# Two decoder layers written out instead of looped, with the expert sum, the next norm and the final scaling done tile by tile

## What is computed

```python
for l in range(DEPTH):                                   # DEPTH = 2
    xp, ... = decoder_layer(xp, 0, ...)                  # 512 prompt rows
    xs, ... = decoder_layer(xs, PAST_LEN, ...)           # 32 sample rows
y_prompt, y_sample = rmsnorm(xp, final_g), rmsnorm(xs, final_g)

def decoder_layer(x, ...):
    h = rmsnorm(x, norm1_g)
    ... = split_cols(h @ w_in)                           # three token mixers:
    #  A gated MLP over chunks, B dilated window attention, C gated delta rule
    #  behind a short convolution over time (state_conv, c_conv_w)
    x = x + concat(out_a, out_b, out_c) @ w_out
    x = x + hier_moe(rmsnorm(x, norm2_g), ...)           # top 2 of 32 experts per token
    return x, ...

def rmsnorm(x, g):
    return x * rsqrt(mean(x * x, -1) + EPS) * g          # in float32
```

## Time and profile before

| | us |
|---|---|
| median of three runs | 1950.37 |
| the profiled execution | 1945.06 |
| its span, first to last instruction | 1943.1 |
| PE busy in it | 1553.9 (80%) |
| DVE, ACT, POOL busy | 621.2, 400.6, 169.7 |
| convR of layer 1 starts | 27.09 |
| first expert sum of layer 1, of layer 2 | 949.57, 1906.63 |
| convR of layer 2 starts | 982.47 |

### The profile page before, as it was taken

How to read it: one execution, slowest core, us unless ns; L and a number is a source line. 1 busy time by engine, 2 the same in 40 slices (tenths; PEclk the granted TensorE clock), 3 DMA queues, 4 the chain that set the end, 5 groups by cost and what they waited for, 6 DMA issues and landing times. The chain is left out here.

```text
span 1943.1 us, 31857 instructions
## 1 busy us (share of the span) xinstructions
PE 1553.9 (80%) x12956; PEld 1020.3 (53%) x12956; DVE 621.2 (32%) x1587; ACT 400.6 (21%) x955; POOL 169.7 (9%) x211
## 2 busy tenths in 40 slices
PE   6999978887679597878399998888785896978880
PEld 3476566765445354544155765667653454544450
DVE  2433155665113211111245322566541132111113
ACT  3221122322311111111131212223232110111111
POOL 0000000000000322222000000000000012222210
PEclk9999998895789699999799989889867897999995
DMA  7152010002862599999440511000047535999984
GB/s 274 45 177 80 1 36 2 2 18 58 226 236 79 170 390 394 397 395 401 151 143 10 189 58 35 2 2 2 20 121 223 197 124 216 387 398 394 397 336 155
DMA packets 97141, 337.13 MB, mean 174 GB/s; under 512 B 33325, under 2 KB 44941, under 8 KB 72317
## 3 DMA queue, kind: packets, MB, share of 16 engines
q1 hardware_dynamic: 77484, 307.86, 44.0%
q0 software_dynamic: 13296, 25.98, 3.9%
q10 hardware_dynamic: 6240, 1.57, 0.4%
HBM read 313.25 MB, written 37.83 MB: 181 GB/s over the span
## 5 line engine op out<-in xcount | busy, mean ns | idle before, releaser
L1587 PE MATMUL bank<-ring,proj_raw 128*64 128x256 f32 x2048 | 264.2, 411 | 79.9 <-DMA ring<-in_w 77.0
L1587 PEld LDWEIGHTS bank<-ring,proj_raw 128*64 128x64 f32 x2048 | 168.8, 143 | 156.2 <-issue 94.9
L1362 PE MATMUL bank<-ring,hT_raw 128*128 128x384 f32 (+2 forms) x768 | 229.2, 462 | 0.0
L1362 PEld LDWEIGHTS bank<-ring,hT_raw 128*128 128x128 f32 x768 | 149.0, 195 | 78.0 <-issue 4.8
L2175 DVE TENSOR_TENSOR qkv_raw<-qkv_raw,bank 128x128 f32<-128x128 f32 x64 | 18.4, 287 | 446.9 <-ACT qkv_raw L1022 446.9
L1299 PE MATMUL bank<-hT_raw,ring 128*128 128x512 f32 x288 | 127.6, 596 | 0.0
L1608 PE MATMUL bank<-ring,proj_raw 128*64 128x512 f32 x512 | 123.9, 604 | 1.5 <-issue 1.5
L1507 PE MATMUL bank<-ring,hT_raw 128*128 128x512 f32 x256 | 113.6, 597 | 0.0
L1080 PE MATMUL bank<-work 64*64 64x64 f32 (+1 forms) x1608 | 73.1, 256 | 37.6 <-DVE work L1730 26.2
L1574 PE MATMUL bank<-consts,proj_raw 64*128 64x64 f32 x512 | 70.1, 278 | 29.0 <-DMA proj_raw<-h_rows,idx 29.0
L1080 PEld LDWEIGHTS bank<-work 64*64 64x64 f32 (+1 forms) x1608 | 66.7, 168 | 47.0 <-DVE work L1730 29.5
(11 more groups left out here) (312 smaller groups left out, 1988.8 us busy)
## 6 DMA issues: line engine op xcount, KB each, us to landing
ring<-in_w SPq DMA_DIRECT2D x192, 1024.0 KB, 18.5
ring<-in_w_in SPq DMA_DIRECT2D x10, 1536.0 KB, 15.1
ring<-in_cache_win_k SPq DMA_DIRECT2D x16, 768.0 KB, 8.7
ring<-in_cache_win_v SPq DMA_DIRECT2D x16, 768.0 KB, 13.7
ring<-in_cache_win_k SPq DMA_DIRECT2D x16, 576.0 KB, 6.9
ring<-in_cache_win_v SPq DMA_DIRECT2D x16, 576.0 KB, 11.1
ring<-in_w_out SPq DMA_DIRECT2D x4, 2048.0 KB, 11.7
h_rows<-proj_raw SPq DMA_DIRECT2D x16, 512.0 KB, 3.6
```

Of the source, the lines that this page charges most:

```text
L1362: mm = pe.matmul(bank[0:ROWS[t], 0:w.shape[2]], hT[:, k, 128 * t:128 * t + ROWS[t]], w[:, k, :], start=k == 0, stop=k == KT - 1)
L1587: mm = pe.matmul(bank[CAP * j:CAP * j + CAP, 0:256].rearrange("p (w f) -> p w f", w=2), rowsT[k % 2][:, CAP * c:CAP * c + CAP], w13[:, :, ...
```

## The change

Each engine's program is written out for both layers, with a set of semaphores for each layer; `leave_layer` is gone. The entry into a norm is one routine on ACT and one on DVE that run tile by tile; it serves both layers and the final norm. On SP the first two `w_in` parts of layer 2 are loaded when experts 29 and 30 have left their slots, the third behind the ten gathers, and the taps and convolution state behind that, once tile 0's sum has read `got[0]` and `got[1]`. `final_g` is loaded ahead of the last gathers into another buffer, and each scaled tile has its own store. `hst` moves in `qkv_raw`. The expert loops, the projections and the mixers keep their code.

```diff
-        hst = [qkv_raw[:, D * i:D * i + D] for i in range(2)]
+        hst = [qkv_raw[:, D * (3 + i):D * (3 + i) + D] for i in range(2)]
-        g_final = proj_raw[:, 0:D]
+        g_final = work[:, 0:D]
-        def leave_layer(eng, L, clears=False):
-            eng.drain().then_inc(layer_left, 1)
-            eng.wait_ge(layer_left, (L + 1) * 5)
...
# SP
-            with sp.Fori(0, DEPTH) as L:
-                sp.dma_start(g1, lay["norm1_g"]...).then_inc(gain_loaded, 16)
-                sp.dma_start(state_rows[0:24, :], ...).then_inc(taps_loaded, 16)
-                sp.dma_start(state_rows[24:28, :], ...).then_inc(taps_loaded, 16)
-                for n in range(3):
-                    stream(L, n, loads[n](L, n % 3))
+            gain_load(0)
+            conv_loads(0)
+            for n in range(3):
+                stream(0, n, loads[n](0, n))
+            for L in range(DEPTH):
...
+                if L + 1 < DEPTH:
+                    gain_load(L + 1)
+                    for n in range(2):
+                        sp.wait_ge(s.act_filled, A0 + 2 * (NE - 3 + n) + 2)
+                        stream(L + 1, n, loads[n](L + 1, n))
+                else:
+                    sp.dma_start(g_final, ...).then_inc(fin_gain, 16)
+                dense_loads(sp, s, L)
                 for k in range(3):
+                    sp.wait_ge(rows_stored[k], 16 * (L + 1) * per_buffer[k] + 16)
                 for t in range(NT):
                     for k in range(2):
                         sp.dma_start(got[2 * t + k]..., y_rows...)
-                dense_loads(sp, L)
-                leave_layer(sp, L)
+                if L + 1 < DEPTH:
+                    stream(L + 1, 2, loads[2](L + 1, 2))
+                    sp.wait_ge(got_used, L * NT + 1)
+                    conv_loads(L + 1)
-            sp.wait_ge(fin_row, NT)
-            sp.dma_start(outs["y_prompt"]..., x[:, 0:NP, :])
+            for t in range(NT):
+                sp.wait_ge(fin_row, t + 1)
+                    sp.dma_start(outs["y_prompt"]...[t], x[:, t, :])
# ACT
+            def enter(L):
+                for t in range(NT + 1):
+                    if t < NT:
+                        if L:
+                            act.wait_ge(got_used, (L - 1) * NT + t + 1)
+                        act.activation(junk1..., x[0:ROWS[t], t, :], ACT.Square, accum_out=ssq...).then_inc(row_squared, 1)
+                    if t >= 1:
+                        u = t - 1
+                        act.wait_ge(row_asked, L * NT + u + 1)
+                        act.activation(rstd[:, u:u + 1], rstd[:, u:u + 1], ACT.Sqrt).then_inc(row_root, 1)
+                        if L < DEPTH:
+                            if u >= 2:
+                                act.wait_ge(of_layer[L].vec_filled, V_AT[("norm1", u - 2, 1)] + 1)
+                            act.activation(hst[u % 2]..., x[...], ACT.Copy, scale=rstd...).then_inc(of_layer[L].rows_ready, 1)
# PE
+                if L:
+                    pe.wait_ge(of_layer[L - 1].act_drained, A0 + 2 * NE)
+                    pe.wait_ge(of_layer[L - 1].vec_drained, V0 + 2 * NE)
# DVE
+            def joined(L, t):           # the two expert sums of tile t, each behind its gather
+            def asked_root(L, t):       # ssq of tile t to mean + EPS, reciprocal, row_asked
+            def enter(L, normed):
+                for t in range(NT + 2):
+                    if L and t < NT:
+                        joined(L - 1, t)
+                    if 1 <= t <= NT:
+                        asked_root(L, t - 1)
+                    if t >= 2:
+                        normed(t - 2)
...
+            enter(DEPTH, finished)      # finished(t): x times the root times final_g
```

More of the change, by code:

```diff
@@ L495, in build @@
+        of_layer = [Signals(L) for L in range(DEPTH)]
         a_jobs, v_jobs = schedule()
@@ L840, in _ @@
+            for L in range(DEPTH):
+                s = of_layer[L]
+                steps, roots, asked = [0], [0], [0]
+                enter(L)
                 bank = get(("tapsT",))
-                act.activation(taps, bank[:, 0:NCT * 28].rearrange("p (c n) -> p c n", c=NCT), ACT.Copy).then_inc(act_drained, 1)
+                act.activation(taps, bank[:, 0:NCT * 28].rearrange("p (c n) -> p c n", c=NCT), ACT.Copy).then_inc(s.act_drained, 1)
                 for i in range(NCT + 1):
```

744 lines of the change are left out of this document (363 added, 381 removed).

## The result

The changed kernel takes 1934.01 us (median of 5 runs, 1927.87 to 1938.93), the kernel before in the same series 1950.37 (5 runs, 1946.23 to 1954.27): a ratio of 0.9916, interval 0.9889 to 0.9942. It is faster by 16.4 us, where 11.8 was forecast, and 1934.01 lies in the range (1930.5 to 1944.0). A second series of both kernels gives a ratio of 0.9945, which is 10.7 us. The changed kernel's profiled execution took 1934.01 us too, with a span of 1932.2; 1933.3 was forecast for it.

A forecast was written before the change was run, and what follows sets the result against it. The prediction took the experts' up projection, waiting for expert weights, as costliest and unchanged. End 12.3, passage 0.6 and start -1.1 sum to 11.8 us: 1950.37 to 1938.6, range 1930.5 to 1944.

The forecast's parts named there:

- The end: First expert sum of layer 2 to the last row: running by tile gains 12.3 us, bounds 9 and 14.
- the 8.8: At the end, from sums' end to first scaling: 8.8 us of the gain, holding the meeting and final_g's load.
- the loop's jump: Between the layers: the jump's instruction fetch costs 3.9 us, won by written-out code but hidden behind the taps.
- The passage: First expert sum of layer 1 to convR of layer 2: gains 0.6 us, bounds -4 and +8.
- the landing of the taps: In the passage: taps, behind gathers and w_in, reach PE at 964.4 instead of 972.00.
- The bound of 4.6: Layer 1's last expert row store, slowed by w_in beside it: bounds 0 and 4.6 us, 0.8 taken.
- The clock: At convR of layer 2: a low clock would cost 1.4 us; half, 0.8, was counted.
- The start: Up to convR of layer 1: tile-wise order loses 1.1 us, bounds 0.5 and 2.
- The middles: Each layer's convR to its first expert sum, 922.5 and 924.2 us: zero change, 1.5 us either side.
- The passage flows: Rival, in the passage: taps early enough, DVE alone sets it, 24.5 us; total 1931; chance 0.18.
- Hand-overs cost: Rival: ACT and DVE requests per tile, 15 tiles, lose 4.5 us; 1945; chance 0.17 with no overlap at the end.
- A starved engine: Rival: written-out code's fetches late under expert loads, 4.6 us each time; four times give 1945 to 1957; chance 0.05.

The follow-up runs named there:

- Old_end: Changed kernel with only the end put back as before, but without the meeting; 1941.11 us, ratio 0.9976 to the kernel before.
- loads_behind: Changed kernel with taps and state right behind the ten gathers and all three w_in parts behind them; 1926.07 us, ratio 0.9899 to the kernel before.
- all_four: all_three plus the edit of sums_first, all ten DVE sums ahead of tile 0's gain; 1914.86 us, ratio 0.9837 to the kernel before.
- rep_after: The changed kernel run once more without any edit; 1932.75 us, ratio 0.9945 to the kernel before.
- sums_first: Changed kernel with all ten DVE sums and the means of tiles 0 to 3 ahead of tile 0's gain in the passage; 1927.84 us, ratio 0.9892.
- all_three: Changed kernel with early taps, all w_in parts behind the gathers, and all squares and root requests first at the start; 1920.34 us, ratio 0.9861.
- before_again: The kernel before, unchanged, profiled once more to see how its stages vary; 1943.32 us in one run.
- early_taps: Changed kernel with taps and convolution state loaded before the experts into a free buffer; 1921.11 us, ratio 0.9874 to the kernel before.
- all_three_again: all_three run once more without further edit; 1919.72 us, ratio 0.9876 to the kernel before.

## Why the prediction was right, and where it was not

**The end: right, and under-sized.** 12.3 forecast; 14.0 from the first sum (36.5 to 22.5), 14.5 from the last store. DVE's row of work was 20.1 us instead of 21.2, and the last store's end came 2.4 behind it instead of 3. The hops between dependent operations were free, which was my bound of 14. Old_end shows that both the meeting and the tiles count. But the meeting is worth 3 to 4.5 us, not the larger part of the 8.8 that I had put down to it and the load of `final_g`. No run separates the loop's jump, for which the prediction named 3.9 us, from the meeting.

**The passage: wrong in one step, the landing of the taps.** It was to gain 0.6 us and lost 5.1 from the last row store to convR. The step that failed is the time at which the taps reach PE. Predicted 964.4 - 943.24 = 21.2 us behind the last row store; measured 28.2. What follows the taps was right: 16.7 forecast, 16.2 measured (985.16 - 969.01), DVE's standstill before tile 3's sums included. The 7.0 us divide so:

- The gathers start 5.12 us behind the store's issue, I had 3.4: 1.8. The bound of 4.6 held; loads_behind shows 2.95 where no `w_in` flows.
- The gathers flow at 258 and 322 GB/s, where as far behind their start it was 338 and 412 before. Over eight us these are 0.68 MB less, at 412 GB/s 1.7 us.
- Then, from 959 to 965, `w_in` and what is left of the gathers move 221 and 287 GB/s at a DMA share above 1, where I had reckoned with the 365 of the earlier trace rows: 1.52 MB in 6 us instead of in 4.2, 1.8.
- The tail, state and taps behind `w_in` in small packets, share 0.77 and 214 GB/s in the last window: 1.7, which is not measured but what is left.

The rates are measured, their cause is not: no run changes the size of the packets alone. The low rate of the third stretch also shows in all_four (257 GB/s in 963:967, with no state or taps behind), so it isn't they who make it. The Trainium skill's rule that descriptors start in order within a queue ("DMA: Bandwidth & Descriptors", "Two DMAs through the same engine are not ordered") agrees with the traces: in the changed kernel, in rep_after and in sums_first the small taps land behind all of `w_in`. The order was right and the rates too high.

**The clock: half counted, twice the price.** I took 0.8, half of 1.4, for a low clock at convR. It was low in all nine executions whose passage ran tile by tile, and took 10.1 to 11.5 us from convR to the second long projection; it was full in all four where the transposes of at least three tiles ran in one piece (both of before, sums_first, all_four), which took 8.7. That is 1.4 to 2.8 us, mostly above what the earlier trace rows had shown, since the clock came back later. At the start, which I hadn't given any of this, tile-wise transposes had a low clock in four executions of six (1.3 to 2.8 us), the others in none of seven. That DVE's order decides it in the passage is shown by sums_first against the changed kernel and all_four against all_three, which differ in nothing else; that it does so by way of PE's pieces is what the timelines suggest. At the start the same pieces went either way, so there they don't decide it alone. "TensorE: Matmul & The Clock Gate" of the Trainium skill says in "Part 1: The HAM clock gate" that the default is throttled and activity releases it; the rows of the passage agree (0.50 while PE stands, 1.00 behind its transposes). At the start the profile has no clock record ahead of the first change, and windows there print 1.00 from the first microsecond on. The durations say otherwise: eight transposes take 1.97 us at first, as at 0.50 in the passage, and 1.16 later.

**The start: right in sign, over-sized.** 1.1 was forecast for convR, with 0.5 and 2 as bounds. Measured are 0.8, 0.3 in the repeat, and over the six executions with this start 0.0 to 0.8, 0.4 in the mean. What the start really lost stands behind convR, in the clock.

**The middles: my 1.5 us were too narrow.** Over the eleven executions with written-out layers they are 899.6 to 912.1. Their means, 906.6 and 904.9, lie 1.0 and 3.8 below those of before (907.7 and 908.8, two profiles that agree within 0.3). By what I had set down ahead of before_again this would be a gain of the change. The clock records of the traces speak against it. PE has the lower of its two clock levels for 174 to 208 us of such a middle, and the length goes with that (correlation 0.93 in layer 1, 0.96 in layer 2): for each us more at the lower level a middle is 0.34 us longer in layer 1 and 0.38 in layer 2. With this taken out, the middles spread by only 1.1 and 0.8 us (standard deviation). Layer 2 of before had the lower level for 195 and 205 us, the written-out ones for 188 in the mean. These 12 us at 0.38 are 4.6, so its 3.8 us are no more than the clock accounts for. In layer 1 before had 188 us, the changed kernel 177.5, which is 3.5 of its 4.8 us. At the same clock before is still some 2 us longer in layer 1, and shorter by 0.7 in layer 2; whether the written-out code has a part in that, or in how the clock is granted, stays open.

**The sum** came out well partly by luck. Against the forecast's terms the end gave 2.2 more and the middles 6.4 that weren't forecast, while the passage to the second long projection lost 8.2 and the start 1.3 more. The prediction itself had divided the kernel elsewhere, at convR and at the first expert sum. Divided so, the changed kernel's profile gives 13.9 for the end (12.3 forecast), -1.9 for the passage (+0.6), -0.8 for the start (-1.1) and -0.4 for the middles (0), in all 10.8. This looks closer, because the shorter middle of layer 1 then hides the late gathers and the slow clock of the start: its 922.5 us before and after are the same by chance, and over the eleven executions they are 921.6 to 929.8. The 5.3 us that I carried over from the profile to the median didn't come back either, since the changed kernel's profile lies at its median.

**The rivals.** "The passage flows" didn't come true for the changed kernel, which takes 34.8 us from first sum to convR. Where the taps are early it nearly has the price that I gave it, 24.5: early_taps takes 25.8, all_three 25.5. With the sums in a block 4 less are enough, 20.5 in all_four. "Hand-overs cost" falls with old_end and sums_first. "A starved engine" has nothing for it: instruction fetches went from 90 packets to 87, and in the mean neither middle became longer.

## What to carry to other kernels

When a loop over layers is written out, list what each queue issues across the seam and ask where the smallest transfer that someone waits for ends up; a buffer of its own for 126 KB was worth 9.5 us of convR, where the whole passage had been expected to give 0.6. Running tile by tile pays where the last consumer is a store (the end), and costs where an in-order engine has work of the same tiles left and stands behind a gain that isn't ready: there put all that needs no answer first. Look at the granted clock ahead of the next dense stretch, since pieces of matmul work with gaps handed it a low clock in all nine such passages here and in four of six starts.

## What the runs showed of the hardware

- SP's issue of a transfer can take long where much stands ahead of it: 4.13 us for the 108 KB of the state in the changed kernel, 0.34 in loads_behind, where only the gathers did, 0.36 and 0.75 in the two profiles of before. Ten gathers took 4.8 to 7.3 us to issue.
- A 64-row indirect store with a `w_in` part beside it was followed by the gathers after 5.0 to 5.3 us in all seven such executions, without it after 2.6 to 3.4 (both of before, loads_behind, all_three, all_four), once after 4.3 (all_three_again).
- A DMA share above 1 doesn't mean full rate: 221, 257, 287, 373 and 420 GB/s all stood beside shares of 1.03 to 1.06.
- The same 16 matmuls of the first long projection took 7.13 us at full clock and up to 8.66 where the clock rose inside them; convR 1.53 and 2.79.
